# Indexer stage of a hybrid attention layer: every engine's order of work written as a table of turns

## What is computed

```python
r = relu(einsum('bqhe,ble->bqhl', qi, ki_all))
score = where(adm, einsum('bqhl,bqh->bql', r, wi), -inf)   # adm: chunk-causal
_, idx = lax.top_k(score, topk)                            # topk = 256
```

## Time and profile before

| | us |
|---|---|
| median of 3 runs (5091.01 to 5095.07) | 5093.04 |
| the profiled execution's own time | 5096.76 |
| its span | 5095.0 |
| TensorE busy | 4347.4 (85%) |
| VectorE busy | 3499.8 (69%) |
| ScalarE busy | 3443.3 (68%) |
| GpSimd busy | 1619.9 (32%) |
| mean granted TensorE clock | 0.92 |

### The profile page before, as it was taken

One profiled execution on the slowest core, in us unless ns is written; L12 is line 12 of the kernel. 1 busy time (PEld: TensorE's weight loads), 2 busy tenths in 40 slices (PEclk: granted clock), 3 DMA queues, 4 the chain that ended last, 5 costly groups with the idle time before them and its releaser, 6 DMA issues. The chain is left out here.

```text
span 5095.0 us, 78325 instructions
## 1 busy us (share of the span) xinstructions
PE 4347.4 (85%) x26505; PEld 2718.1 (53%) x26505; DVE 3499.8 (69%) x6644; ACT 3443.3 (68%) x6887; POOL 1619.9 (32%) x1358
## 2 busy tenths in 40 slices
PE   6777888777677786767689999989999999989999
PEld 3344444434343343434366777767777777754444
DVE  1277779888797898989477777787777778625111
ACT  1588888888787798872488888858788885520100
POOL 1345566667557757777210000000000000000000
PEclk8888889888788898978799999999999999999999
DMA  5211111100010111101421111011010010044422
GB/s 143 70 44 45 38 39 40 37 35 28 33 42 33 37 45 38 36 32 48 157 72 58 44 51 40 28 54 41 25 42 25 28 40 26 10 126 132 117 93 103
DMA packets 201975, 276.98 MB, mean 54 GB/s; under 512 B 50496, under 2 KB 134176, under 8 KB 201056
## 3 DMA queue, kind: packets, MB, share of 16 engines
q1 hardware_dynamic: 198624, 271.81, 16.9%
q10 hardware_dynamic: 2960, 0.17, 0.0%
HBM read 156.73 MB, written 114.16 MB: 53 GB/s over the span
## 5 line engine op out<-in xcount | busy, mean ns | idle before, releaser
L596 PE MATMUL bank<-w,x 128*128 128x512 f32 (+1 forms) x2848 | 1258.6, 598 | 19.2 <-DVE w L941 12.8
L1043 DVE TENSOR_SCALAR_CACHE_REDUCE ties<-score,cand 128x512 int8<-128x512 f32 (+13 forms) x448 | 1110.6, 2479 | 122.1 <-POOL score L917 106.7
L596 PEld LDWEIGHTS bank<-w,x 128*128 128x128 f32 x2848 | 576.9, 206 | 608.6 <-issue 549.7
L807 ACT ACTIVATE act_junk<-score,a_cand,a_sign 128x384 int8<-128x384 f32 (+13 forms) x420 | 879.4, 2094 | 14.0
L614 PE MATMUL bank<-kiT,qi 128*128 128x512 f32 (+3 forms) x1136 | 396.5, 489 | 450.5 <-ACT relu L737 244.9
L1834 DVE CUSTOM_DVE_ANT_0 row<-bank,mask 128x512 f32<-128x512 f32 (+3 forms) x1024 | 622.6, 639 | 181.6 <-PE bank L1573 180.3
L1540 POOL TENSOR_TENSOR near_bias<-table,mask 128x2048 f32<-128x2048 f32 (+1 forms) x32 | 129.5, 4047 | 1767.8 <-DVE part L1834 1751.4
L1768 ACT ACTIVATE pT<-bank 128x512 f32<-128x512 f32 (+2 forms) x704 | 368.4, 523 | 428.5 <-PE bank L1589 426.6
L1670 ACT ACTIVATE row<-row,top 128x1024 f32<-128x1024 f32 (+7 forms) x640 | 632.9, 990 | 4.0 <-DVE top L1847 4.0
L1573 PE MATMUL bank<-kT,qb 64*128 64x256 f32 (+1 forms) x4352 | 609.6, 397 | 9.0 <-DVE part L1834 5.6
L1589 PE MATMUL bank<-ident,row 128*128 128x128 f32 x4224 | 594.6, 281 | 26.4 <-DVE pT L1945 19.6
(11 more groups left out here) (255 smaller groups left out, 4900.1 us busy)
## 6 DMA issues: line engine op xcount, KB each, us to landing
qk_t<-ring SPq DMA_DIRECT2D x66, 256.0 KB, 2.0
gates<-ring SPq DMA_DIRECT2D x66, 256.0 KB, 2.0
gate<-gates SPq DMA_DIRECT2D x33, 512.0 KB, 3.4
out<-x_in SPq DMA_DIRECT2D x33, 512.0 KB, 2.9
x<-in_x_prompt SPq DMA_DIRECT2D x32, 512.0 KB, 3.7
mixed<-mixT SPq DMA_DIRECT2D x64, 256.0 KB, 2.0
mix_in<-mixed SPq DMA_DIRECT2D x32, 512.0 KB, 4.3
x_in<-in_x_prompt SPq DMA_DIRECT2D x32, 512.0 KB, 3.8
```

What stands on the lines that cost most here:

```text
L596: ins = pe.matmul(p_bank[n % 2][:, 0:n1 - n0], held[:, c * P:(c + 1) * P], w[:, c, n0:n1], start=(c == 0), stop=(c == KC - 1))
L807: tick(act.activation(junk, row, ACT.Sign, bias=c, scale=back, accum_out=a_sum[:, :]))
L1043: n = tick(dve.tensor_scalar(ties[:, 0:width], row, c.bitcast(F32), 0.0, ALU.is_ge, ALU.add, accum_out=counts[:, i:i + 1]))
```

## The change

The planner (`test_us` to `FAR_AWAY`, `RELU_GAP`) goes, and so do the slots of TensorE and GpSimd. Each engine's work becomes two to five generators, "lines of work", that keep their own order, and a table of turns says which line has the next turn. A letter is a line, the number how many turns it takes in a row:

```diff
+def in_turn(text):
+    return [(word[0], int(word[1:] or 1)) for word in text.split()]
...
+def take_turns(order, **work):
+    for kind, many in order:
+        for _ in range(many):
+            next(work[kind])
+    for left in work.values():
+        assert next(left, None) is None
...
+DVE_TURNS = in_turn("""
+w26 h q w8 h q h q h q s4 h s4 q s19 h c q s11 h s q s16 h s3 q s9 c h s q s3 h s10 q s8 h s7 c s6 q s8 h s6 q s14 h
+c s6 q s7 h s8 q s11 h s2 c s6 q s6 h s8 q s9 h s c s10 q s6 h s9 q s7 h c s12 q s5 h s10 q s7 c h s12 q s5 h s11 q
+s2 c h s14 q s2 h s13 q s4 c h s13 q s5 h s13 q c s h s14 q s5 h s11 c q s4 h s13 q s6 h s11 c q s4 h s15 q s4 h s11
+c q s3 h s20
+""")
...
-            def background():
-
-                taken = 2
-                for t in range(TILES + 5):
-                    for slot in (0, 3, 6, 9, 11):
-                        while taken < SEARCHED and FOUND_AT[taken] <= us_at(t, slot):
-                            yield FOUND_AT[taken]
-                            choose_act(taken)
-                            taken += 2
...
+            take_turns(DVE_TURNS, w=weights(), q=splits(), h=heads(), c=closes(), s=searches())
```

The last third of the table of ScalarE, and the last lines of the others:

```diff
+ACT_TURNS = in_turn("""
...
+r s r3 b4 r4 s3 b4 r3 s b4 r3 s b2 r3 s b s r s b r3 s r2 s r2 s r3 s r2 s r2 s b4 r3 s r s r2 b3 r s2 b3 s b2 s b2
+s2 b r2 s b r2 s2 r s r s r3 s r2 s r2 s r2 s r3 s r2 s r5 b4 r4 s3 b4 r3 s b2 r b r2 s b r2 b2 r s2 b r s b r3 s r2
+s r3 s r2 s r2 s r3 s r2 s r2 s b4 r3 s2 r3 s b3 s b3 s b2 s b2 r s r b r s r s b r s r2 s r2 s r2 s r3 s r2 s r2 s
+r3 s r4 b4 r4 b2 r5 b2 r3 b2 r2 b r b r3 b2 r2 b r2 b r4 b2 r2 b r b r7
+""")
+
+POOL_TURNS = in_turn("""
+n7 a5 n2 a4 n a n a5 n a4 n a6 n a3 n a6 n a3 n2 a4 n a4 n a5 n a9 n2 a15 n a5 n a6 n2 a18 n a3 n a9 n2 a19 n a4 n
+a11 n2 a20 n a5 n a13 n2 a24 n a4 n a14 n a3 n a21 n a5 n a17 n a4 n a23 n a2 n a21 n a4 n a22 n a4 n a24 n a5 n a24
+n a4 n a28 n a3 n a23 n a4 n a32 n a3 n a27 n a4 n a37 n a25
+""")
...
+            take_turns(PE_TURNS, t=transposes(), j=projections(), u=scores())
+            take_turns(ACT_TURNS, b=background(), r=relus(), s=searches())
+            take_turns(POOL_TURNS, a=sums(), n=rows())
```

More of the change, by code:

```diff
@@ L127 @@
 SLOTS = 12
-RELU_GAP = 1.8
 BIG = float(2 ** 100)
@@ L216, in step_us @@
[L216 to L257, removed]
@@ L260 @@
[L260 to L268, removed]
@@ L538, in _ @@
             pe.wait_ge(s_rin, 32)
-            pe.matmul(s_bank[0][0:2 * HEADS, 0:383], bias_in, hot_in, start=True, stop=True).then_inc(s_ramp, 1)
             def piece_bank(name, t):
@@ L815, in search @@
                 for h in (64, 32, 16, 8, 4, 2, 1):
-                    test(c)
+                    yield from test(c)
                     if h >= 16:
@@ L853, in search, with searches @@
                 act.activation(found[:, 2:3], sign, ACT.Copy).then_inc(s_found, 1)
-            for a in range(2, SEARCHED, 2):
-                search(a)
-            advance(us_at(TILES + 4, 0))
+                yield
+            def searches():
+                for a in range(2, SEARCHED, 2):
+                    yield from search(a)
+            take_turns(ACT_TURNS, b=background(), r=relus(), s=searches())
         @block.gpsimd
@@ L917, in add_scores, with sums, rows @@
                         pool.memset(row_of(u)[0:CHUNK, width - CHUNK:width], PAD).then_inc(s_sum, 1)
-            scale_row(0)
-            for t in range(TILES + 1):
-                for slot in range(SLOTS):
-                    if 3 <= t:
-                        add_scores(t - 1, slot)
-                    if slot == 5 and t < TILES:
+                        yield
+            def sums():
+                for u in range(2, TILES):
+                    yield from add_scores(u)
+            def rows():
+                scale_row(0)
+                yield
+                for t in range(TILES + 1):
+                    if t < TILES:
                         scale_row(t + 1)
-                    if slot == 8:
-                        norms(t)
+                        yield
+                    norms(t)
+                    yield
+            take_turns(POOL_TURNS, a=sums(), n=rows())
         @block.vector
@@ L1052, in search, with searches @@
                 dve.wait_ge(s_dve, tick.n)
-                n = tick(dve.tensor_reduce(over, counts[:, :], AX.X, ALU.max))
+                n = tick(dve.tensor_reduce(own_over, counts[:, :], AX.X, ALU.max))
                 dve.wait_ge(s_dve, n)
-                n = tick(dve.tensor_scalar(left, over, -1.0, float(TOPK), ALU.mult, ALU.add))
+                n = tick(dve.tensor_scalar(own_left, own_over, -1.0, float(TOPK), ALU.mult, ALU.add))
                 dve.wait_ge(s_dve, n)
-                advance(max(DVE_END[a] - 1.0, FOUND_AT[a - 1]))
-                choose(a, cand[:, TESTS % 2:TESTS % 2 + 1].bitcast(F32))
-            for a in range(3, SEARCHED, 2):
-                search(a)
-            advance(FAR_AWAY - 1)
+                yield
+                choose(a, cand[:, TESTS % 2:TESTS % 2 + 1].bitcast(F32), own_left)
+                yield
+            def searches():
+                for a in range(3, SEARCHED, 2):
+                    yield from search(a)
+            take_turns(DVE_TURNS, w=weights(), q=splits(), h=heads(), c=closes(), s=searches())
 CHOICE_STEPS = 31 * 3 + 20
```

244 lines of the change are left out of this document (138 added, 106 removed).

## The result

| | us |
|---|---|
| after, median of 4 runs (4874.99 to 4880.94) | 4880.1 |
| before, median of 4 runs on the same chip (5091.01 to 5097.89) | 5094.06 |
| ratio, 95% interval | 0.9578 [0.9561, 0.9594] |
| the profiled execution's own time | 4880.94 |
| its span | 4879.1 |

A forecast was written before the change was run, and what follows sets the result against it. Bound: the ring of three rows with the written places of relus and even closings, VectorE's own work just behind. Terms 65 + 17 + 10 + 25 = 117 us off 5096.8 gave 4980, predicted as 4975; range 4900 to 5060.

The forecast's parts named there:

- Early: Stage one up to 765 us: ScalarE sets the pace, 10 us gained, between -60 and +40.
- The limit "+40": Upper bound, in us, on the gain forecast for stage one up to 765 us.
- The first rival: Searches of 3 to 13: later even closings hold rows longer, costing 80 us; time 5148, chance 9%.
- Late: Searches 19 to 27, 1206 to 2207 us: earlier closings and relus remove waits, 65 us gained, between about 0 and 95.
- for dearer closings: Searches 19 to 27: VectorE's even closings slow down beside a busy GpSimd, 3 us in each of five turns.
- Middle: Searches 13 to 17, 765 to 1206 us: two thirds of VectorE's 25.6 us row waits go, 17 us gained, 0 to 40.
- end: 2207 to 2456 us: closing 28 sooner lets row 31 end before VectorE; 25 of 38 us gained, 0 to 32.
- GpSimd takes the wait: Rival: GpSimd, locked out 14 us a closing, makes rows as late as before; 45 us off, 5048, chance 13%.
- The price of 14 us: Late even closings: GpSimd loses some 14 us each, blocked under VectorE's passes.
- Cost at nothing: Two added columns, a second wait in transpose_ik, moved SyncE stores and the first matmul's place: no time counted.
- What would show it: Signs: stage two at 2340 +- 20, late searches about 205 us apart, GpSimd idle under 10 us before a row.

The follow-up runs named there:

- half_old: Order of the kernel before, with half of the products of the projections of tiles 2 to 9 left out; 5064.86 us.
- kv_first: Order of the kernel before, but for tiles 2 to 9 TensorE multiplies group kv of the next tile ahead of the first score unit; 5070.0 us, ratio 0.9954.
- replay_old: The changed kernel with its five tables replaced by ones that write out the order of the kernel before; 5094.66 us, ratio 0.9999.

## Why the prediction was wrong, and where it was right

*Early, the step that failed.* The prediction said that ScalarE "is busy 492 of 578 us from 187 on the earlier trace rows and sets the pace; it waits 35.4 us for TensorE's groups, which the change moves by one or two groups", and took 10 us. What failed is the size of that wait's part: it was judged by the places in TensorE's table alone, while ScalarE's own copies, relus and tests changed places too. ScalarE's waits in 187 to 765 us before (the line of 35.4 us stands in the earlier trace rows):

```profile
ACT weight L696 <- PE bank L596: 10.1, 3, 3.6
...
ACT act_junk L796 <- POOL score L917: 8.8, 2, 4.9
```

and in 163 to 687 us after:

```profile
ACT relu L739 <- POOL score L915: 10.0, 6, 3.7
ACT proj L704 <- PE bank L603: 2.2, 4, 0.7
...
ACT weight L700 <- PE bank L603: 0.2, 1, 0.2
```

Its waits for TensorE's groups went from 45.5 us (35.4 + 10.1) to 2.4, and all its listed waits from 67.8 to 17.3: that is the 50 us by which its idle time fell, from 86 to 35. Which of the moved turns took them away is open; half_old and kv_first show that less or sooner work on TensorE alone gives 29 and 24 us.

VectorE's wait for whole rows taken by itself would have misled here: it rose from 13.1 to 53.9 us in the stretch that became 50 us shorter. Its wait for ScalarE's copies went the other way, from 97.7 to 28.7 us, and no row of the prediction had looked at it. Before, then after:

```profile
DVE ties L946 <- ACT proj L700: 97.7, 7, 26.0
...
DVE ties L1043 <- POOL score L917: 13.1, 3, 7.4
```

```profile
DVE ties L1043 <- POOL score L920: 53.9, 6, 17.3
DVE ties L960 <- ACT proj L704: 28.7, 3, 25.0
```

The other 28 of the 78 us are the start. Row 2 was whole at 163.88 us before, but the search began at 187.21, behind copies that waited for TensorE:

```profile
181.07 0.69 ACT L700 ACTIVATE proj<-bank,row_scale 128x512 f32<-128x512 f32 x1 [5.00 <-PE bank L596]
...
185.90 0.26 ACT L696 ACTIVATE weight<-bank,row_scale 128x4 f32<-128x4 f32 x1 [3.65 <-PE bank L596]
...
187.21 0.62 ACT L796 ACTIVATE act_junk<-score,a_const 128x384 int8<-128x384 f32 x1
```

After, it starts at 163.53. The prediction did not look at this stretch. The limit "+40" on the gain had no row under it; the 86 us of ScalarE's idle time and the 23 us between the whole row 2 and its search would have been one that the trace gives.

*The first rival, later early closings cost 80 us.* Wrong in sign. In the new order the odd search starts closer behind the even one: 34 us for 8 and 9 (422 and 456), 52 before (459 and 512). ScalarE's result therefore falls later in the odd search, and a closing behind 28 tests is where it comes. Closing by the old counts costs 70 us. I had counted places in the list, from the start of one search, and not the time between two searches.

*Late.* 65 forecast, 77 measured. The waits of 52.1 and 42.8 us went down to 5.9 and 25.5, with 11.1 new. The 3 us a turn "for dearer closings" came for tiles 24 and 26 only (8.30 for 7.36 in the scan of 26, 4.90 for 3.82 behind it); the scans of 18 and 20 took 5.22 and 5.76 us as before. And the odd closings became cheaper, with fewer of GpSimd's adds beside them now: the scan of 27 took 7.62 after 8.57. The two scans of one turn, by lines, before and after:

```profile
L972 DVE TENSOR_TENSOR_SCAN score<-ties 128x3456 f32<-128x3456 int8 (+1 forms) x2 | 15.9, 7966 | 0.1
```

```profile
L986 DVE TENSOR_TENSOR_SCAN score<-ties 128x3456 f32<-128x3456 int8 (+1 forms) x2 | 15.9, 7963 | 0.1
```

Over all ten closings of the five turns VectorE's five wide passes took 180.2 us after 186.4, so the 15 us of that term were not there. And the gain is not where I put it: 27 to 29 takes 216.1 us, not 205 (220.8 before), and a ScalarE turn of row 26 to 28 takes 211.1, not 182 (214.0). The gain lies in 19 to 23, 320 us instead of 375, where ScalarE is busy 311 and VectorE 305 us of 320.

*Middle and end.* 17 forecast and 27 measured, though VectorE still waits 19.4 us for whole rows there (25.6 in the earlier trace rows). Its wait for copied projections, which the term left out, fell from 17.4 to 0.6 us. That the forecast came near is luck in part: the wait that the 17 was taken from gave 6. At the end 25 and 29. Behind the last mask 4.5 us are left, as said.

*GpSimd takes the wait.* The lockouts came and did not decide: row 29 is whole 29 us early. The price of 14 us held in the closing of 26: the three operations took 8.09, 4.55 and 4.66 us, 17.3 in all, where such operations take 1.04, 1.04 and 1.27 by the median, 3.35 in all. But it did not come on top of what was there: GpSimd's adds and multiplications of the five turns took 580 us after 601 before, for nearly the same number.

*Cost at nothing* was right (replay_old).

*What would show it* held for VectorE's wait for rows, for ScalarE's result (5.1 us at most in one closing), for the wait of the relus and for the end of the stage. It did not hold for the start of stage two (2245, not 2340 +- 20), for the distance of the searches of 27 and 29 (216, not 205), for GpSimd's idle time ahead of a row (some 15 us, not under 10) and for the number of its long operations (9 after 11, not twice as many).

What stays open: which of the moved turns took away ScalarE's early waits; how far the 77 us of the late stretch part into closings and relus, since the closings alone make the kernel slower and no run moves the relus alone; and whether an order exists that fills ScalarE and VectorE in the turns of 25 to 29, where VectorE still has 20 us idle in 216.

## What to carry to other kernels

Where several engines work through fixed lists around a ring of buffers, bound what a new order can bring by the whole idle time of the fullest engine in each stretch, and not by one of its waits, judged by its place in one other engine's list; here the stretches gave back 50 of 86 us early and 77 of 133 late. Count a moved wait by the time at which its result comes, not by its place in a list; a wait placed too early can be paid by the engines behind it too. A part of an order need not give a part of its gain: two mixtures of the two orders were 52 and 195 us slower than the old one, where the whole new order gained 214.

## What the runs showed of the hardware

The time of a closing depends on whether GpSimd is adding beside it, and both sides pay: VectorE's scan of 3456 columns took 7.36 us beside an idle GpSimd and 8.30 beside a busy one, and the GpSimd operation beside it 8.09 instead of 1.04. Moved from odd to even tiles, the cost left VectorE's sum where it was (3499.8 and 3502.0 us).

In the first stretch TensorE's granted clock was 0.93 of 2.4 GHz (a mean between its two levels) with the engine busy 465 of 524 us, against 0.87 with 446 of 578 before; the fuller order went with the faster clock. With half of the products left out of the new order it was 0.88, at 407 busy of 524 us, and the kernel no slower; this speaks against the clock as the source of the early gain, but does not exclude it, since TensorE had less to do in that run.
